# A hybrid decoder step in fp32 on one core: head sums shared between two engines, and cached values summed four units at a time

## The chip, the core and the metric

One NeuronCore of a Trainium2 chip runs the whole kernel as one program. The metric is the device time of one execution in microseconds (us). TensorE, VectorE, ScalarE, GpSimd and SyncE are the core's engines; the profile calls them PE, DVE, ACT, POOL and SP. Each runs its own list of instructions in order, and they wait for each other by semaphores alone.

## The reference

One layer of a hybrid decoder, for 256 prompt tokens and for 8 sequences of 4 new tokens that look back at 2048 cached positions each (288 tokens in all, width 2048):

```
h = rmsnorm(x);  q,k,v, qi,ki,wi, cx,cb,cc, ga,gb = split(h @ w_in)
score = sum over 16 index heads of wi * relu(qi . ki)        # picks keys
idx   = top_k(score)            # 64 for the prompt, 256 for the samples
logit[h,j] = q[h] . k[idx[j],h] / sqrt(128) + rel_bias       # 8 heads of 128
attn  = softmax(logit) @ v[idx]          # rows come from a paged cache
m = sigmoid(ga) * (attn @ w_pa) + sigmoid(gb) * ((cb * conv(cc*cx)) @ w_pb)
x = x + m @ w_o;  x = x + relu(rmsnorm(x) @ w1)**2 @ w2;  y = rmsnorm(x)
```

For the samples each of the 32 queries picks 256 keys of its own. Key rows and value rows (8 heads x 128 numbers, 4 KB) are fetched from HBM by their picked positions.

## The kernel before

**Projections.** Every fp32 product is made of three: a weight tile is split into a high half (VH, a rounded copy) and a low half (VL, the rest), the activations likewise, and TensorE adds high*high, high*low and low*high (lines 428 to 430). The input projection runs over 44 *pairs* of 256 output columns (`win_half`), each pair over eight *chunks* u of two 128-row tiles: 12 matmuls a chunk. So chunk number u runs from 0 to 351, pair p is chunks 8p to 8p+7. For each chunk SyncE loads weights into `wring`, ScalarE copies VH (`highs`, up to four chunks ahead of TensorE, line 932), and VectorE or GpSimd subtracts VL (`lows`, lines 1281 and 1834). `dve_low(u)` (line 77) says which: in the key stage VectorE has chunks 2 and 6 of eight, in the value stage the odd ones, and GpSimd the others. After the projections come the mixing, output and MLP products, which the change does not touch (there `WH` and `WL` play the same parts).

All else is hung between those chunks by hand: `win_half(p, half, after)` calls `after(j)` behind chunk j, and every other engine places its own work by `highs(end)` or `lows(end)`, "first all halves below chunk `end`, then this".

**Picking.** VectorE finds the 256 best keys of each sample query, four positions to a *unit*: 64 units, and in each of them partition 4n+s of 128 works for query n and its key s. `comb` holds positions by query. `picked` (line 707) spreads them over 128 partitions by four matmuls with the 0/1 matrices `rs`; `bias_at(0)` (line 735) does the same for the new tokens' column. VectorE turns positions into row numbers `offs` (lines 1495 to 1506).

**Key stage (pairs 15 to 30).** GpSimd gathers one unit of key rows (128 rows of 4 KB, 512 KB) into one of `RK` = 5 buffers of `kv` (`gather`, line 1843), once the unit five earlier has been read. VectorE multiplies the unit by the queries in PSUM banks 6 and 7 (`by_query`, line 1521) and sums each head's 128 products (`by_head`, line 1525) into the logits `lg`. Units are paced by `unit_end(n)` (line 73): 1.9 chunks a unit.

```
for n in range(UNITS):
    dve.wait_ge(ks[n % RK], 16 * (n // RK + 1))
    by_query(kv[:, n % RK, :])
    by_head(kv[:, n % RK, :], lg[:, n, :])
    lows(unit_end(n) + 4)
```

GpSimd's side (line 1859): `lows(unit_end(n - RK) + 4 or 5)`, then `gather(n)`. Small work of VectorE stands between units: four `one_hot`, four `gated` products, the new token's keys in `knrep` (unit 35, summed at unit 41). The prompt's own top 64 takes eight rounds of `prompt_top` (line 1486): two before the units, six in pair 31.

**Value stage (pairs 31 to 38).** After the softmax VectorE spreads each unit's probabilities into one of two tiles `sp` (`spread_unit`, line 1597), and after every second chunk TensorE multiplies two units of value rows by them (`unit_sum` and `v_unit`, lines 835 to 846): per unit 8 heads, in fp32 two passes each, so 16 small matmuls. `vnrep` (the new tokens' values) comes first. The value rows use the same five buffers. Between the halves of a pair stand the prompt's attention products, and VectorE has its softmax rows and the convolution.

Of the kernel before, what the change touches and what calls it, by code (L numbers as in the profile page):

```python
# [59 lines left out]
           ("iota", NPG), ("tpos", 1), ("nd", DT), ("lo", NB), ("npos", DT), ("par", 1)]  # L60
# [5 lines left out]
NEWKEY = 35  # L66
RAW = 3
# [5 lines left out]
def unit_end(n):  # L73
    return 8 * KP + (3 + 19 * n // 5) // 2
# [44 lines left out]
def build(nc, I, O):  # L119
    with ExitStack() as ctx:  # L120
# [54 lines left out]
        sp = sb("sp", [P, 2, H, NS])  # L175
# [89 lines left out]
        def const(name, rows=P):  # L265
# [19 lines left out]
            "unit_read conv_done soft_ready soft_turned lg_shifted lg_exp "  # L285
            "sp_ready unit_summed o_copied ot_done ot_copied "
            "ul_ready ul_turned ul_copied u_out res_add relu_raw y_turned y_copied y_squared ssy_sum root_ready y_out "
# [3 lines left out]
        ks = [ctx.enter_context(nc.semaphore(f"rows_in{i}")) for i in range(RK)]  # L291
# [8 lines left out]
        C_MLP = C_WO + 16  # L300

# [102 lines left out]
        def _(pe):  # L404
# [495 lines left out]
        def _(act):  # L900
# [258 lines left out]
            for p in range(VP, AP0 + H + 1):  # L1159
# [20 lines left out]
                if p == VP + UNITS // UNIT:  # L1180
                    act.wait_ge(S["ot_done"], 1)
                    copy(zB[:, 0:H, SEQ:TOK], bank(6, 0, H * NS).rearrange("p (h n) -> p h n", h=H)).then_inc(S["ot_copied"], 1)
            act.activation(XH[:, 0:CT, :], zB[:, CT:KT, :], ACT.Copy).then_inc(S["xh_ready"], 1)
            gate(AP0 + H + 1)
            act.wait_ge(S["ot_copied"], 1)
# [69 lines left out]
            act.wait_ge(S["ssy_sum"], 1)  # L1255
            act.activation(root3, ssq, ACT.Sqrt, bias=eps[:, 0:1], scale=1.0 / D).then_inc(S["rms_ready"], 1)
            act.wait_ge(S["root_ready"], 1)
# [11 lines left out]
        def _(dve):  # L1269
# [257 lines left out]

            dve.wait_ge(S["q_wide"], 2)
# [14 lines left out]
            for n in range(UNITS):  # L1543
                dve.wait_ge(ks[n % RK], 16 * (n // RK + 1))
                by_query(kv[:, n % RK, :])
                by_head(kv[:, n % RK, :], lg[:, n, :])
# [3 lines left out]
                elif n == 10:  # L1550
                    dve.wait_ge(S["spread_done"], 3)
                    dve.tensor_scalar(newsel[:], bank(4, 0, 1), -1.0, -OFF, ALU.add, ALU.mult).then_inc(S["newpos_read"], 1)
# [6 lines left out]
                elif n == NEWKEY + 6:  # L1559
# [3 lines left out]
                    step(dve.scalar_tensor_tensor(out=rnew, in0=qstep_k[:], scalar=QKS, in1=rnew, op0=ALU.mult, op1=ALU.add))  # L1563
                if turn < 24 and unit_end(n) > UNIT * turn + UNIT:
# [10 lines left out]
            dve.wait_ge(S["unit_read"], UNITS + 1)  # L1575
            dve.wait_ge(S["bias_copied"], 1)
# [215 lines left out]
            for e in range(2):  # L1792
# [10 lines left out]
                if e:  # L1803
                    dve.tensor_reduce(ssq, ssy, AX_X, ALU.add).then_inc(S["ssy_sum"], 1)
# [4 lines left out]
            dve.wait_ge(S["ssy_sum"], 1)  # L1809
# [5 lines left out]
            dve.scalar_tensor_tensor(out=root3, in0=half3, scalar=1.5, in1=root3, op0=ALU.add, op1=ALU.mult).then_inc(S["root_ready"], 1)  # L1815
            dve.wait_ge(S["root_ready"], 1)
# [7 lines left out]
        def _(pool):  # L1824
# [18 lines left out]
            def gather(n):  # L1843

                src, u = ("cache_k", n) if n < UNITS else ("cache_v", n - UNITS)
                if RK <= n < UNITS + RK:
                    pool.wait_ge(S["unit_read"], n - RK + 1 + (n - RK > NEWKEY + 6))
                elif n >= UNITS + RK:
                    pool.wait_ge(S["unit_summed"], u - RK + 2)
                pool.indirect_dma_start(out=kv[:, n % RK, :], out_offset=None, in_=I[src],  # L1850
                                        in_offset=bass.IndirectOffsetOnAxis(ap=offs[:, u:u + 1], axis=0)).then_inc(ks[n % RK], 16)
# [7 lines left out]
            for n in range(UNITS + RK):  # L1859
                lows(UNIT * KP + 4 + n if n < RK else unit_end(n - RK) + (5 if NEWKEY < n - RK < NEWKEY + 10 else 4))  # L1860
# [25 lines left out]
            pool.wait_ge(S["root_ready"], 1)  # L1886
# [4 lines left out]
def constants():  # L1891
# [11 lines left out]
    c["s32"] = (p[:, None] // 4 == n32[None, :])  # L1903
    c["b4"] = (p[:, None] // 4 == p[None, :] // 4)
# [77 lines left out]
```

## Time and profile before

| | us |
|---|---|
| median of 3 runs (1751.91 to 1753.06) | 1752.29 |
| the profiled execution | 1752.91 |
| its span, first to last instruction | 1751.1 |
| TensorE busy | 1722.1 |
| VectorE, ScalarE, GpSimd busy | 1050.5, 684.5, 535.1 |
| mean granted clock of TensorE | 0.995 of full |

The profile shows one execution. A matmul's record overlaps the next one's, since they are pipelined: its duration is some 0.29 us while a new one starts every 0.13 us, so rates are read from starts and counts. `<-` behind an idle time names what ended it. A window line gives, for a stretch, each engine's busy time and instruction count, the clock granted to TensorE, the busy share of the 16 DMA engines and what they moved. Measured from the span's start, the key stage is about 254 to 476 us and the value stage 483 to 640 us.

### The profile page before, as it was taken

What the parts mean: (1) busy time and instruction counts of PE and PEld (TensorE: products, weight loads), DVE (VectorE), ACT (ScalarE), POOL (GpSimd) and SP (SyncE); (2) the same over time, 40 slices, a digit from 0 to 9 for tenths busy, and PEclk for the clock granted to TensorE, in tenths of its full rate; (3) what the DMA queues carried; (4) which work ended last, traced back from release to release, by engine and by line L of the source; (5) the groups of instructions that cost most, each with busy time, mean ns of one, the idle gap of its engine ahead of it and who ended that gap; (6) DMA issues with size and microseconds to landing.
All of it is one profiled execution on the core that took longest, in us unless ns stands there. A gap on an engine that the chain in (4) does not pass through costs nothing.

```text
span 1751.1 us, 32532 instructions
## 1 busy us (share of the span) xinstructions
PE 1722.1 (98%) x13708; PEld 1684.4 (96%) x13708; DVE 1050.5 (60%) x1185; ACT 684.5 (39%) x846; POOL 535.1 (31%) x430
## 2 busy tenths in 40 slices
PE   9999999999999999999999999999999999999997
PEld 9879999999989999999999999999999999999997
DVE  5979999799897422555556544455444554445444
ACT  5544443434435555333333332233333333333342
POOL 1647788898967668000340000000000000000000
PEclk9999999999999999999999999999999999999998
DMA  8635558998979965644454444444444444444442
GB/s 314 208 95 181 175 179 304 347 335 309 315 264 344 325 233 155 224 168 164 159 184 166 168 167 159 160 163 168 168 167 161 159 163 166 168 169 162 154 165 103
DMA packets 74816, 351.86 MB, mean 201 GB/s; under 512 B 8978, under 2 KB 11154, under 8 KB 53684
## 3 DMA queue, kind: packets, MB, share of 16 engines
q1 hardware_dynamic: 50352, 269.05, 45.2%
q0 software_dynamic: 19584, 71.31, 11.5%
q10 hardware_dynamic: 4772, 9.95, 1.7%
q8 instruction: 81, 1.33, 0.3%
q14 instruction: 27, 0.22, 0.0%
HBM read 343.84 MB, written 6.44 MB: 200 GB/s over the span
## 4 chain that ended last, share of the span: by engine, by line
PE 81%; DVE 15%; POOL 1%; DMA 1%; issue 1%; ACT 0%; ACTq 0%; DVEq 0%
PE PM L448 20%; PE PM L450 19%; PE PM L449 19%; PE PM L428 6%; PE PM L429 6%; PE PM L430 6%; DVE ix L1464 2%; DVE scw L1466 2%; DVE scw L1463 2%; PE PM L410 2%; PE PM L838 2%; DVE kv L1523 1%; DVE VL L1287 1%; DVE lg L1526 1%; POOL kv L1850 1%
## 5 line engine op out<-in xcount | busy, mean ns | idle before, releaser
L905 ACT ACTIVATE WH<-wring 128x2048 fp32r<-128x2048 f32 (+1 forms) x163 | 307.3, 1885 | 679.9 <-PE PM L450 676.1
L1693 DVE TENSOR_TENSOR WL<-wring,WH 128x2048 fp32r<-128x2048 f32 x159 | 364.5, 2292 | 341.0 <-ACT WH L905 341.0
L1840 POOL TENSOR_TENSOR VL<-wring,VH 128x512 fp32r<-128x512 f32 x273 | 358.0, 1320 | 160.7 <-ACT VH L905 157.2
L428 PE MATMUL PM<-hH,VH 128*128 128x288 f32 x1312 | 398.2, 304 | 7.8 <-DVE VL L1287 4.4
L429 PE MATMUL PM<-hL,VH 128*128 128x288 f32 x1312 | 388.5, 296 | 0.0
L430 PE MATMUL PM<-hH,VL 128*128 128x288 f32 x1312 | 387.0, 295 | 0.0
L448 PE MATMUL PM<-XH,WH 128*128 128x288 f32 x1280 | 379.1, 296 | 1.5 <-DVE WL L1700 1.5
L449 PE MATMUL PM<-XL,WH 128*128 128x288 f32 x1280 | 377.6, 295 | 0.0
L450 PE MATMUL PM<-XH,WL 128*128 128x288 f32 x1280 | 376.3, 294 | 0.0
L448 PE MATMUL PM<-YH,WH 128*128 128x288 f32 x1264 | 374.6, 296 | 0.0
L449 PE MATMUL PM<-YL,WH 128*128 128x288 f32 x1264 | 372.9, 295 | 0.0
L450 PE MATMUL PM<-YH,WL 128*128 128x288 f32 x1264 | 371.6, 294 | 0.0
L905 ACT ACTIVATE VH<-wring 128x512 fp32r<-128x512 f32 x352 | 221.4, 631 | 319.8 <-PE PM L430 311.4
L428 PEld LDWEIGHTS PM<-hH,VH 128*128 128x128 f32 x1312 | 247.1, 188 | 18.2 <-issue 7.8
L1888 POOL TENSOR_SCALAR ysam<-ysam,small 32x512 f32<-32x512 f32 x1 | 2.4, 2372 | 823.0 <-DVE small L1815 823.0
L430 PEld LDWEIGHTS PM<-hH,VL 128*128 128x128 f32 x1312 | 248.3, 189 | 0.0
L429 PEld LDWEIGHTS PM<-hL,VH 128*128 128x128 f32 x1312 | 247.8, 189 | 0.2
L448 PEld LDWEIGHTS PM<-XH,WH 128*128 128x128 f32 x1280 | 239.8, 187 | 1.8 <-ACT G L993 1.7
L450 PEld LDWEIGHTS PM<-XH,WL 128*128 128x128 f32 x1280 | 241.1, 188 | 0.0
L449 PEld LDWEIGHTS PM<-XL,WH 128*128 128x128 f32 x1280 | 240.3, 188 | 0.1
L450 PEld LDWEIGHTS PM<-YH,WL 128*128 128x128 f32 x1264 | 238.1, 188 | 0.0
L449 PEld LDWEIGHTS PM<-YL,WH 128*128 128x128 f32 x1264 | 237.3, 188 | 0.0
(293 smaller groups left out, 1704.6 us busy)
## 6 DMA issues: line engine op xcount, KB each, us to landing
wring<-w_in SPq DMA_DIRECT2D x176, 512.0 KB, 4.6
wring<-w_mlp_in SPq DMA_DIRECT2D x64, 1024.0 KB, 5.2
wring<-w_mlp_out SPq DMA_DIRECT2D x64, 1024.0 KB, 5.2
wring<-w_o SPq DMA_DIRECT2D x16, 1024.0 KB, 5.2
wring<-w_pb SPq DMA_DIRECT2D x8, 1024.0 KB, 4.8
wring<-w_pa SPq DMA_DIRECT2D x8, 1024.0 KB
xT<-x_t SPq DMA_DIRECT2D x1, 2304.0 KB, 11.1
kv<-x_prompt SPq DMA_DIRECT2D x2, 1024.0 KB, 8.3
```

What stands on the lines that cost most here:

```text
L410: return pe.transpose(out, in_, cp[0:n, 0:n])
L428: pe.matmul(out, vh, th[:, k, :], start=(k == 0), stop=False)
L429: pe.matmul(out, vh, tl[:, k, :], start=False, stop=False)
L430: m = pe.matmul(out, vl, th[:, k, :], start=False, stop=(k == KT - 1))
L448: pe.matmul(out, wh, rh[:, k0 + k, :], start=(first and k == 0), stop=False)
L449: pe.matmul(out, wh, rl_[:, k0 + k, :], start=False, stop=False)
L450: m = pe.matmul(out, wl, rh[:, k0 + k, :], start=False, stop=(last and k == CK - 1))
L838: m = pe.matmul(PM[q:q + NS, 6, c:c + HD], sp[:, ring, h, :], rows[:, h * HD:h * HD + HD], start=(first and h < 4), stop=False, skip_group ...
L905: return act.activation(out, in_, ACT.Copy, **kw)
L1463: step(dve.max(v8, sc2))
L1693: dve.tensor_tensor(WL[:, i % 2], wring[:, i % 2], WH[:, i % 2], ALU.subtract).then_inc(S["wl_ready"], 1)
L1840: pool.tensor_tensor(VL[:, u % 4], r, VH[:, u % 4], ALU.subtract).then_inc(S["vl_pool"], 1)
```

## The change

1. **Heads shared.** For the 28 units 5, 7, ..., 59 (`SHARED`) VectorE multiplies the half with heads 4 to 7 first, then the half with heads 0 to 3, and sums only heads 0 to 3. ScalarE sums heads 4 to 7 by four copies with accumulation, placed behind the VH copy of chunk `unit_end(n) + 4`. A gather over such a unit waits for ScalarE too.
2. **Prompt tops** 2 to 7 move from pair 31 to units 6, 9, 12, 15, 18 and 21.
3. **Spreading** of `comb` by one matmul with `rall` (all four positions to all partitions) instead of four with `rs`; VectorE then picks each partition's own with a 0/1 constant `sel` and a sum.
4. **Gathers** follow `lows(unit_end(n - RK) + 6)`; the first eight follow one chunk each.
5. **Values** are summed four units at a time, after chunks 3 and 7 of a pair, with four `sp` tiles and seven row buffers: the five of `kv`, `knrep` and `vnrep`.
6. Some semaphores are merged (`norm_step`, `o_copied`).

```diff
+SHARED = range(5, 60, 2)
+TOPS_AT = (6, 9, 12, 15, 18, 21)
-        sp = sb("sp", [P, 2, H, NS])
+        sp = sb("sp", [P, 4, H, NS])
+        def v_row(v):
+            r = v % (RK + 2)
+            if r < RK:
+                at = (UNITS + r) % RK
+                return kv[:, at, :], ks[at], 16 * (-(-(UNITS - at) // RK) + v // (RK + 2) + 1)
+            return (knrep if r == RK else vnrep)[:], ks[r], 16 * (v // (RK + 2) + 1)
 # TensorE
-                    for s in range(4):
-                        m = pe.matmul(bank(4, 0, UNITS), const("rs", NS)[:, s * P:s * P + P], comb[:, 0:UNITS, s],
-                                      start=(s == 0), stop=(s == 3))
-                    m.then_inc(S["spread_done"], 1)
+                    pe.matmul(bank(4, 0, TOPK), const("rall", NS), comb[:, 0:UNITS, :].rearrange("p u s -> p (u s)"),
+                              start=True, stop=True).then_inc(S["spread_done"], 1)
...
-                    for s in range(4):
-                        m = pe.matmul(bank(4, 0, 1), const("rs", NS)[:, s * P:s * P + P], comb[:, UNITS, s:s + 1],
-                                      start=(s == 0), stop=(s == 3))
-                    m.then_inc(S["spread_done"], 1)
+                    pe.matmul(bank(4, 0, 4), const("rall", NS), comb[:, UNITS, :],
+                              start=True, stop=True).then_inc(S["spread_done"], 1)
...
             def v_unit(v):
-                n = UNITS + v
+                rows, arrived, count = v_row(v)
                 pe.wait_ge(S["sp_ready"], v + 2)
-                pe.wait_ge(ks[n % RK], 16 * (n // RK + 1))
-                unit_sum((1 + v) % 2, kv[:, n % RK, :])
+                pe.wait_ge(arrived, count)
+                unit_sum((1 + v) % 4, rows)
...
-                    if j % 2 and v < UNITS:
-                        v_unit(v - 1)
-                        v_unit(v)
+                    if j == 3 and v < UNITS:
+                        for i in range(4):
+                            v_unit(v - 3 + i)
 # ScalarE
+            def unit_heads(n):
+                act.wait_ge(S["unit_made"], SHARED.index(n) + 1)
+                for h in range(H // 2, H):
+                    row = kv[:, n % RK, h * HD:h * HD + HD]
+                    m = act.activation(row, row, ACT.Copy, accum_out=lg[:, n, h:h + 1])
+                m.then_inc(S["unit_act"], 1)
+            shared_at = {unit_end(n) + 4: n for n in SHARED}
             def highs(end):
...
                     copy(VH[:, u % 4], raw[u // 2 % 4][:, 2 * (u % 2):2 * (u % 2) + 2, :]).then_inc(S["vh_ready"], 1)
+                    if u in shared_at:
+                        unit_heads(shared_at[u])
 # VectorE
-            pw = bank(4, 0, UNITS)
+            pw, every = bank(4, TOPK, UNITS), view(scw, 0, [UNITS, 4])
+            step(dve.tensor_tensor(every, bank(4, 0, TOPK).rearrange("p (u s) -> p u s", s=4),
+                                   const("sel").unsqueeze(1).to_broadcast([P, UNITS, 4]), ALU.mult))
+            step(dve.tensor_reduce(pw, every, AX_X, ALU.add))
...
+            def half_unit(rows, out):
+                for e in (1, 0):
+                    part = rows[:, 512 * e:512 * e + 512]
+                    m = dve.tensor_tensor(part, part, PM[:, 6 + e, :], ALU.mult)
+                    if e:
+                        m.then_inc(S["unit_made"], 1)
+                    else:
+                        step(m)
+                dve.tensor_reduce(out, rows[:, 0:512].rearrange("p (h d) -> p h d", h=H // 2), AX_X, ALU.add).then_inc(S["unit_read"], 1)
...
-                by_query(kv[:, n % RK, :])
-                by_head(kv[:, n % RK, :], lg[:, n, :])
+                if n in SHARED:
+                    half_unit(kv[:, n % RK, :], lg[:, n, 0:H // 2])
+                else:
+                    by_query(kv[:, n % RK, :])
+                    by_head(kv[:, n % RK, :], lg[:, n, :])
                 lows(unit_end(n) + 4)
...
+                if n in TOPS_AT:
+                    prompt_top(2 + TOPS_AT.index(n))
...
-                if v:
-                    dve.wait_ge(S["unit_summed"], v)
-                spread((1 + v) % 2, lg[:, v, :].unsqueeze(2).to_broadcast([P, H, NS]))
+                if v >= 3:
+                    dve.wait_ge(S["unit_summed"], v - 2)
+                spread((1 + v) % 4, lg[:, v, :].unsqueeze(2).to_broadcast([P, H, NS]))
...
-                    if c % 2 == 0 and v < UNITS:
-                        spread_unit(v)
-                        spread_unit(v + 1)
+                    if c % 4 == 0 and v < UNITS:
+                        for i in range(4):
+                            spread_unit(v + i)
                     lows(UNIT * p + c + 4)
                     if p == VP:
-                        if c < TOPP // 8 - 2:
-                            prompt_top(c + 2)
 # GpSimd
             for n in range(UNITS + RK):
-                lows(UNIT * KP + 4 + n if n < RK else unit_end(n - RK) + (5 if NEWKEY < n - RK < NEWKEY + 10 else 4))
+                lows(UNIT * KP + 4 + n if n < RK + 3 else unit_end(n - RK) + 6)
                 gather(n)
...
-            for v in range(0, UNITS - RK):
-                lows(UNIT * VP + v + 5)
-                gather(UNITS + RK + v)
+            for v in range(RK, UNITS):
+                if v == RK:
+                    pool.wait_ge(S["unit_read"], UNITS + 1)
+                else:
+                    lows(UNIT * VP + v - 2)
+                    pool.wait_ge(S["unit_summed"], v - RK)
+                gather_v(v)
```

## Rows read from the trace of the kernel before

**Rows 1.** Page, busy us (share of the span) xinstructions
```profile
PE 1722.1 (98%) x13708; PEld 1684.4 (96%) x13708; DVE 1050.5 (60%) x1185; ACT 684.5 (39%) x846; POOL 535.1 (31%) x430
```

**Rows 2.** Waits of TensorE, whole run: us in total, times, longest
```profile
PE PM L428 <- DVE VL L1287: 5.4, 5, 2.4
PE PM L428 <- POOL VL L1840: 3.0, 3, 2.2
PE PM L838 <- DVE sp L1595: 2.6, 4, 0.8
```

**Rows 3.** Windows: us, busy (x) of each engine, PEclk, DMA share, GB/s
```profile
430.00:455.66 25.66, 25.66 (x194) 25.66 (x194) 23.66 (x22) 11.21 (x18) 23.69 (x21) 1.00 0.92 321
547.44:566.65 19.21, 19.21 (x236) 17.65 (x235) 8.23 (x20) 9.91 (x17) 12.98 (x13) 1.00 0.92 327
```

**Rows 4.** Windows of TensorE alone: us, busy (x), PEclk, DMA share, GB/s
```profile
260.00:270.00 10.00, 6.90 (x45) 0.96 0.90 304
270.00:280.00 10.00, 10.00 (x69) 0.87 0.96 341
390.00:400.00 10.00, 9.07 (x67) 1.00 0.91 320
400.00:410.00 10.00, 9.40 (x71) 1.00 0.87 304
410.00:420.00 10.00, 8.24 (x50) 0.83 0.85 279
470.00:480.00 10.00, 8.93 (x66) 1.00 0.89 315
```

**Rows 5.** Timeline of TensorE, value stage: start us, us, engine line op
```profile
498.29 1.08 PE L838 MATMUL PM<-kv,sp 128*32 128x128 f32 x32 [0.82 <-DVE sp L1595]
...
547.22 0.29 PE L430 MATMUL PM<-hH,VL 128*128 128x288 f32 x1
547.44 1.08 PE L838 MATMUL PM<-kv,sp 128*32 128x128 f32 x32
548.45 0.40 PE L428 MATMUL PM<-hH,VH 128*128 128x288 f32 x1
```

**Rows 6.** Timeline of TensorE's weight loads, same visit
```profile
547.44 0.81 PEld L838 LDWEIGHTS PM<-kv,sp 128*32 128x32 f32 x32 [0.17 <-issue]
```

**Rows 7.** Timeline of VectorE, key stage and value stage
```profile
316.31 0.69 DVE L1287 TENSOR_TENSOR VL<-wring,VH 128x512 fp32r<-128x512 f32 x1 [1.80 <-ACT VH L905]
316.92 1.22 DVE L1523 TENSOR_TENSOR kv<-kv,PM 128x1024 f32<-128x1024 f32 x1
318.17 1.22 DVE L1526 TENSOR_REDUCE lg<-kv 128x8 f32<-128x1024 f32 x1
...
488.37 0.28 DVE L1489 MAX8 m8p<-mask 128x8 f32<-128x128 f32 x1
...
490.05 0.29 DVE L1489 MAX8 m8p<-mask 128x8 f32<-128x128 f32 x1
...
511.68 0.41 DVE L1614 TENSOR_REDUCE qstep<-scw 128x1 f32<-128x256 f32 x1
```

**Rows 8.** Timeline of ScalarE, value stage
```profile
512.12 0.40 ACT L1145 ACTIVATE scw<-scw,qstep 128x128 f32<-128x128 f32 x1 [1.39 <-DVE qstep L1614]
...
512.52 0.49 ACT L1145 ACTIVATE scw<-scw,qstep 128x256 f32<-128x256 f32 x1
```

**Rows 9.** Timeline of GpSimd, key stage
```profile
267.32 1.27 POOL L1840 TENSOR_TENSOR VL<-wring,VH 128x512 fp32r<-128x512 f32 x1
...
304.89 0.96 POOL L1850 DMA_INDIRECT kv<-cache_k,offs  x1
```

**Rows 10.** Timeline of TensorE, the two blocks that spread `comb`
```profile
245.51 1.18 PE L711 MATMUL PM<-comb,cp 32*128 32x64 f32 x8
...
286.23 1.05 PE L740 MATMUL PM<-comb,cp 32*128 32x1 f32 x8
```

**Rows 11.** Gathers of line 1850, from issue to landing
```profile
DMA to landing us min/median/max: 4.8/6.7/9.0
```

More of the change, by code:

```diff
@@ L59 @@
 CONST_P = [("ident", P), ("rs", 4 * P), ("rall", P), ("s32", NS), ("b4", P), ("ok4", 4),
-           ("iota", NPG), ("tpos", 1), ("nd", DT), ("lo", NB), ("npos", DT), ("par", 1)]
+           ("iota", NPG), ("tpos", 1), ("nd", DT), ("lo", NB), ("npos", DT), ("par", 1), ("sel", 4)]
 CONST_E = [("onehot", TW), ("amask", DB * P), ("causal", 3 * P), ("pgsel", P), ("r8", 1)]
@@ L284, in build @@
             "plog_done plog_read pmax_ready pexp_done pprob_ready pt_turned pt_copied po_done po_copied "
-            "unit_read conv_done soft_ready soft_turned lg_shifted lg_exp "
-            "sp_ready unit_summed o_copied ot_done ot_copied "
-            "ul_ready ul_turned ul_copied u_out res_add relu_raw y_turned y_copied y_squared ssy_sum root_ready y_out "
+            "unit_read unit_made unit_act conv_done soft_ready soft_turned lg_shifted lg_exp "
+            "sp_ready unit_summed o_copied ot_done "
+            "ul_ready ul_turned ul_copied u_out res_add relu_raw y_turned y_copied y_squared norm_step y_out "
             "ptT_in ptT_ready prow_sum prow_ready wh_ready wl_ready xh_ready xl_ready yh_ready yl_ready mix_sum dve_step "
@@ L290, in build @@
         ld = [ctx.enter_context(nc.semaphore(f"weights_in{i}")) for i in range(RING)]
-        ks = [ctx.enter_context(nc.semaphore(f"rows_in{i}")) for i in range(RK)]
+        ks = [ctx.enter_context(nc.semaphore(f"rows_in{i}")) for i in range(RK + 2)]
         pages_in = [ctx.enter_context(nc.semaphore(f"pages_in{i}")) for i in range(DB)]
@@ L1181, in _ @@
                     act.wait_ge(S["ot_done"], 1)
-                    copy(zB[:, 0:H, SEQ:TOK], bank(6, 0, H * NS).rearrange("p (h n) -> p h n", h=H)).then_inc(S["ot_copied"], 1)
+                    copy(zB[:, 0:H, SEQ:TOK], bank(6, 0, H * NS).rearrange("p (h n) -> p h n", h=H)).then_inc(S["o_copied"], 1)
             act.activation(XH[:, 0:CT, :], zB[:, CT:KT, :], ACT.Copy).then_inc(S["xh_ready"], 1)
             gate(AP0 + H + 1)
-            act.wait_ge(S["ot_copied"], 1)
+            act.wait_ge(S["o_copied"], 2)
             act.wait_ge(S["po_copied"], H)
@@ L1254, in _ @@
                 half_squares(e)
-            act.wait_ge(S["ssy_sum"], 1)
+            act.wait_ge(S["norm_step"], 1)
             act.activation(root3, ssq, ACT.Sqrt, bias=eps[:, 0:1], scale=1.0 / D).then_inc(S["rms_ready"], 1)
-            act.wait_ge(S["root_ready"], 1)
+            act.wait_ge(S["norm_step"], 2)
             act.wait_ge(S["y_copied"], 8)
@@ L1551, in _ @@
                     dve.wait_ge(S["spread_done"], 3)
-                    dve.tensor_scalar(newsel[:], bank(4, 0, 1), -1.0, -OFF, ALU.add, ALU.mult).then_inc(S["newpos_read"], 1)
+                    step(dve.tensor_tensor(m8[:, 0:4], bank(4, 0, 4), const("sel"), ALU.mult))
+                    step(dve.tensor_reduce(m8[:, 4:5], m8[:, 0:4], AX_X, ALU.add))
+                    dve.tensor_scalar(newsel[:], m8[:, 4:5], -1.0, -OFF, ALU.add, ALU.mult).then_inc(S["newpos_read"], 1)
                     dve.wait_ge(S["newpos_read"], 1)
@@ L1575, in _ @@
             dve.wait_ge(S["unit_read"], UNITS + 1)
+            dve.wait_ge(S["unit_act"], len(SHARED))
             dve.wait_ge(S["bias_copied"], 1)
@@ L1803, in _ @@
                 if e:
-                    dve.tensor_reduce(ssq, ssy, AX_X, ALU.add).then_inc(S["ssy_sum"], 1)
+                    dve.tensor_reduce(ssq, ssy, AX_X, ALU.add).then_inc(S["norm_step"], 1)
                 m = dve.tensor_tensor(ynat[:, :, c], bank(6).rearrange("p (q n) -> p q n", q=2)[:, :, h],
@@ L1808, in _ @@
                     m.then_inc(S["y_copied"], 1)
-            dve.wait_ge(S["ssy_sum"], 1)
+            dve.wait_ge(S["norm_step"], 1)
             dve.wait_ge(S["rms_ready"], 3)
@@ L1814, in _ @@
             step(dve.tensor_tensor(half3, half3, root3, ALU.mult))
-            dve.scalar_tensor_tensor(out=root3, in0=half3, scalar=1.5, in1=root3, op0=ALU.add, op1=ALU.mult).then_inc(S["root_ready"], 1)
-            dve.wait_ge(S["root_ready"], 1)
+            dve.scalar_tensor_tensor(out=root3, in0=half3, scalar=1.5, in1=root3, op0=ALU.add, op1=ALU.mult).then_inc(S["norm_step"], 1)
+            dve.wait_ge(S["norm_step"], 2)
             dve.wait_ge(S["y_copied"], 8)
@@ L1843, in gather, with gather_v @@
             def gather(n):
[L1845 to L1851, printed above, removed]
+                if n >= RK:
+                    k = n - RK
+                    pool.wait_ge(S["unit_read"], k + 1 + (k > NEWKEY + 6))
+                    if k in SHARED:
+                        pool.wait_ge(S["unit_act"], SHARED.index(k) + 1)
+                if n < UNITS:
+                    pool.indirect_dma_start(out=kv[:, n % RK, :], out_offset=None, in_=I["cache_k"],
+                                            in_offset=bass.IndirectOffsetOnAxis(ap=offs[:, n:n + 1], axis=0)).then_inc(ks[n % RK], 16)
+                else:
+                    gather_v(n - UNITS)
+            def gather_v(v):
+                rows, arrived, _ = v_row(v)
+                pool.indirect_dma_start(out=rows, out_offset=None, in_=I["cache_v"],
+                                        in_offset=bass.IndirectOffsetOnAxis(ap=offs[:, v:v + 1], axis=0)).then_inc(arrived, 16)
             for b in range(DB):
@@ L1864, in _ @@
                     pool.memset(up[:, :, 0:2], 0.0).then_inc(S["pads_zero"], 1)
[L1865 to L1867 removed]
+            for v in range(RK, UNITS):
+                if v == RK:
+                    pool.wait_ge(S["unit_read"], UNITS + 1)
+                else:
+                    lows(UNIT * VP + v - 2)
+                    pool.wait_ge(S["unit_summed"], v - RK)
+                gather_v(v)
             lows(C_MIX)
@@ L1885, in _ @@
             square_pairs(0, 0)
-            pool.wait_ge(S["root_ready"], 1)
+            pool.wait_ge(S["norm_step"], 2)
             pool.wait_ge(S["y_copied"], 8)
@@ L1903, in constants @@
     c["s32"] = (p[:, None] // 4 == n32[None, :])
+    c["sel"] = (p[:, None] % 4 == np.arange(4)[None, :])
     c["b4"] = (p[:, None] // 4 == p[None, :] // 4)
```

## The prediction

> **What bounds the kernel now.** I read the totals first: TensorE is busy 1722.1 of 1751.1 us [rows 1], so all that can be won is a gap between its instructions, or fewer or cheaper instructions. The second view is who waited for whom, TensorE's part: its longest totals are 5.4 us for VectorE's low halves VL, 3.0 us for GpSimd's, 2.6 us for the spread tiles `sp` [rows 2]. Third come its windows. A clean stretch, 430.00 to 455.66, holds 194 matmuls in 25.66 us, 132 ns each [rows 3]. Against that beat of 75.6 matmuls per 10 us the key stage has three holes [rows 4]:
> - its start, 260 to 280 us: 114 matmuls, not 151, so some 4.9 us lost;
> - its middle, 390 to 420 us: 188, not 227: 5.1 us;
> - its end, 470 to 480 us: 66: 1.3 us.
>
> A hole costs more than its wait: the granted clock fell to 0.87 in 270 to 280 and 0.83 in 410 to 420 [rows 4], below the full 2.4 GHz, after waits of up to 2.2 and 2.4 us [rows 2].
>
> **Value stage: groups of four.** A visit to two units is 32 small matmuls: the last projection matmul starts at 547.22, the units at 547.44, the next projection matmul at 548.45 [rows 5]. Against a beat of 0.13 the way in costs 0.09; the way out costs 0.11 (that next matmul ran 0.40, a clean one 0.29); the visit itself 1.01. Of that 1.01, 0.81 is the 32 weight loads back to back [rows 6]; 0.20 is a tail in which nothing issues. So the fixed part is 0.40 us a visit. There are 32 visits of two and there will be 16 of four: 16 x 0.39 = **6.2 us** gained. Were the tail owed by each unit, only the ways in and out would go: 16 x 0.20 = 3.2, my lower bound; nothing supports more than 6.4.
> The rows show the fixed part. The Trainium skill (TensorEngine Tiling (Array Packing), Key Properties) says that changing the tiling mode drains TensorE; by it, a pair of mode changes per visit is what is halved, which gives the 6.2 and not the 3.2.
>
> **Value stage: the waits for `sp`.** Twice before two-unit visits it waited 0.82 us, as at 498.29 [rows 5], and twice inside one, 0.5 each; 2.6 in all [rows 2], plus two tails of a split visit, 0.2 each. They come from six `prompt_top` calls, 1.68 us each (488.37 to 490.05) [rows 7], put between the spreads. Those leave this stage, and with four `sp` buffers the spreads of a group are made while the previous group's four chunks run, some 6 us early. I take **2.8 us**; bounds 2.0 and 3.0. The 1.1 us wait for VL right after the new key's rows stays: four spreads now stand ahead of that subtraction, not two, but the third and fourth fit into the time that the new key's matmuls take.
>
> **Key stage: VectorE.** A unit is a product of 1.22 and a sum of 1.22 us, starting 1.25 apart and 2.39 together [rows 7]. Of 28 units it now makes two half products (a subtraction of 128x512 took 0.69, 0.61 to its successor) and half a sum (128x256 took 0.41 [rows 7], so 128x512 some 0.68, 0.60 issued). That is 0.60 + 0.64 + 0.60 = 1.84: 0.54 saved, 15 us in all. Against it, six tops x 1.71 = 10.3 us move in at units 6 to 21. There VectorE has room: it waits for VH, 1.80 us per two units [rows 7], some 13 us from unit 10 to 24. So the tops are hidden; if that cover were gone they would show as a wait for VL. From unit 23 on, before the middle hole, ten shared units give 5 us, where VectorE was late by 2.4. But gathers are issued two chunks later, and one crowded stretch may eat the lead. I take 1.5 us of the hole as left if so: **3.4 us** gained, bounds 0 and 5.1. At the end VectorE comes 1 us sooner to the softmax: **1.2** of 1.3; bounds 0.5 and 1.3.
>
> **Key stage: ScalarE.** Four sums of 128x128 with accumulation: one, with its read-out, occupied 0.40 us (512.12 to 512.52) [rows 8], so 1.6 us per shared unit, 45 us in 178. ScalarE is 44% busy there (11.21 of 25.66 us) [rows 3]; it becomes about 70%. Queued behind the new wait and sums are the next VH, and behind that GpSimd's and VectorE's VL and TensorE. In 16 chunks of 1.60 us it idles 14.45, 0.9 a chunk, so the next VH comes 0.7 us late, with an evacuation 1.2. VH is made four chunks (6.4 us) ahead, and copy and subtraction need 2, so it is covered. The wait itself ends in time where VectorE is no more than 3 us behind.
>
> **Key stage: GpSimd.** It is the fullest helper: 23.69 of 25.66 us [rows 3]. Its gathers now come after VL two chunks further on. At the start that helps: before, three gathers in a row stood ahead of the VL at 267.32 [rows 9] for which TensorE waited 2.2 us. But all of it starts 0.9 us later: two new operations on 128x256 and 256-to-64 elements (0.43 + 0.45 from the 0.41 of [rows 7]) stand before the row numbers, and TensorE arrives 0.6 us sooner. Following both queues, chunks 125 to 129 each wait 0.6 to 0.9 us for GpSimd and chunk 130 some 2 us for VectorE, which is also 0.9 us late: 7 us lost where 5 were. Term: **-2.0**, bounds -4 and +3.
>
> **Matrix products merged.** Eight passes took 1.18 us busy (1.11 to the next) and 1.05 (0.97) [rows 10]. One matmul of two passes instead: 0.5 for 256 columns, 0.3 for 4. **1.2 us**; bounds 0.6 and 1.6.
>
> **Gathers.** Issued some 3.3 us later, against a lead of 11 us for unit 17 (issued at 304.89 [rows 9], used at 316.92 [rows 7]) and somewhat less later, with landings of 4.8 to 9.0, median 6.7 [rows 11]: VectorE will wait for rows more often, with 3 us before TensorE feels it. In the value stage seven buffers hold one group and three units more, so a burst of four keeps the queue filled. The two new rows are `knrep` and `vnrep`, free by then. For these and small collisions I charge **-1.0** (0 to -4). The renamed semaphores and the last norm cost nothing: the same waits.
>
> **Sum.** 6.2 + 2.8 + 3.4 + 1.2 - 2.0 + 1.2 - 1.0 = 11.8 us. Against the profiled execution (1752.91: span 1751.1 and 1.8 around it) that is 1741.1; it lay 0.6 above the median, so 1740.5. A measurement here tells about 0.2%, 3.5 us, from no change.
>
> **The rivals.**
> - *The tail is per unit* (0.11): 3.0 us less, **1743.5**. Against it: the loads run back to back through both units [rows 6].
> - *The transfers become the bound of the value stage* (0.11). A pair there moves 2.10 MB of weights and 4.19 MB of rows: 327 GB/s at share 0.92 over 19.21 us [rows 3]; full share would be 355, 17.7 us. I ask for 19.2 - 0.8 = 18.4 us, 342 GB/s. If late rows take half of what the groups win, **1744**; the sign would be waits on `kv`, `knrep` or `vnrep`. The Trainium skill (DMA: Bandwidth & Descriptors, Bandwidth) puts a core's HBM share at about 358 GB/s; by that the pair could not be under 17.6 us, still short of a bound.
> - *The start gains from the new order* (0.10): GpSimd's delay matters less than I think, the 2.2 us wait and its slow clock go, and the middle hole closes: **1734**.
> - *Slower: ScalarE's wait for VectorE's half product* (0.07). Place: the VH copy behind each of the 28 waits, at chunk `unit_end(n) + 4`. If rows land so late that the product ends over 3 us after VH, TensorE stops at each: 0.6 us of wait and 0.2 of restart, 28 x 0.8 = 22 us, against 11.8 + 1.0 of gain: **1762**. It decides from about 0.45 us a unit. For it: the later gathers; against: the latest that VectorE has been cost TensorE 2.4 us [rows 2], and it will be earlier.
> - *The sharing does nothing* (0.05), since TensorE waits for VectorE in few places: then groups, `sp` waits and merged products remain less the start: **1744**.
>
> **The numbers.** Forecast 0.56. All but the slower one lie at 1734 to 1744. The range, 1733 to 1747, takes in the start and the middle at their bounds, not the slower rival. Faster by over 0.2% means under 1748.8: 0.88; within: 0.05; slower 0.07.
>
> **What would show it.** Right: value-stage visits of 64 matmuls in about 1.8 us, 18.4 us a pair, no wait for `sp`; one row of ScalarE sums at 0.40; a smaller middle hole; a start with several waits under 1 us. Wrong: waits on ScalarE's VH in the key stage, DMA waits on the rows, or visits of 2.0 us.

## The result, and the profile after

The changed kernel takes **1755.64 us** (median of 20 runs, 1752.96 to 1757.55), the kernel before 1752.55 in the same comparison: ratio 1.0016, 95% interval 1.0010 to 1.0022. I had forecast 1740.5. The profiled execution lies at 1754.53, its span is 1752.7.

**Where the time went.** ScalarE copies each VH at a fixed place in TensorE's work, so the start of the same copy in two traces shows how far one kernel is ahead at a chunk. The changed one against before, in us (+ is behind):

| from chunk to chunk | what lies there | forecast | measured |
|---|---|---|---|
| 112 to 124, 136 to 144 | the two merged products | -1.2 | -0.5, -0.9 |
| 124 to 136 | start of the key stage | +2.0 | +3.9 |
| 144 to 244 | rest of it, the middle hole | -3.4 | -0.8 |
| 244 to 256 | softmax, hand-over | -1.2 | +3.4 |
| 256 to 316 | value stage | -9.0 | -2.8 |

(The -1.0 charged for the gathers belongs to the third line and the last; the changed one was 0.6 us ahead already at chunk 112. The misses: 6.2 us in the value stage, 4.6 at the hand-over from the key stage to it, 2.6 and 1.9 before.) The page's busy times, TensorE's waits [rows 2] and its windows [rows 4]:

```profile
PE 1719.8 (98%) x13696; PEld 1685.7 (96%) x13696; DVE 1068.3 (61%) x1217; ACT 713.6 (41%) x1070; POOL 534.4 (30%) x430
```
```profile
PE PM L438 <- DVE VL L1305: 11.9, 8, 3.6
PE PM L438 <- POOL VL L1877: 2.0, 4, 0.7
```
```profile
260.00:270.00 10.00, 7.74 (x55) 1.00 0.93 323
270.00:280.00 10.00, 6.43 (x39) 0.83 0.88 307
390.00:400.00 10.00, 7.82 (x47) 0.83 0.88 320
...
410.00:420.00 10.00, 10.00 (x77) 1.00 0.89 291
...
480.00:490.00 10.00, 8.21 (x62) 0.83 0.57 197
```

The waits for `sp` are gone, but those for VectorE's VL have grown from 5.4 to 11.9 us. The start is worse (39 matmuls in 270 to 280, there were 69), the middle hole has only moved from 409 to 391 (its wait is 2.2 us, it was 2.4), and there is a new one at 480. The granted clock is at 0.83 in each of the three. The four longest waits in the timeline of TensorE, and a visit of four units:

```profile
274.64 0.40 PE L438 MATMUL PM<-hH,VH 128*128 128x288 f32 x1 [3.57 <-DVE VL L1305]
...
393.74 0.40 PE L438 MATMUL PM<-hH,VH 128*128 128x288 f32 x1 [2.18 <-DVE VL L1305]
...
482.84 0.40 PE L438 MATMUL PM<-hH,VH 128*128 128x288 f32 x1 [1.79 <-DVE VL L1305]
...
542.71 0.40 PE L438 MATMUL PM<-hH,VH 128*128 128x288 f32 x1 [1.46 <-DVE VL L1305]
...
582.43 1.96 PE L844 MATMUL PM<-kv,sp 128*32 128x128 f32 x64
584.31 0.70 PE L820 MATMUL PM<-scw,G 128*128 128x256 f32 x2
```

What VectorE did just before each, from its timeline:

```profile
272.35 2.24 DVE L1305 TENSOR_TENSOR VL<-wring,VH 128x512 fp32r<-128x512 f32 x1
...
390.31 3.37 DVE L1305 TENSOR_TENSOR VL<-wring,VH 128x512 fp32r<-128x512 f32 x1
...
479.91 2.87 DVE L1305 TENSOR_TENSOR VL<-wring,VH 128x512 fp32r<-128x512 f32 x1
...
538.90 3.16 DVE L1634 TENSOR_TENSOR sp<-cp,lg 128x256 f32<-128x256 f32 x4
541.98 0.68 DVE L1305 TENSOR_TENSOR VL<-wring,VH 128x512 fp32r<-128x512 f32 x1
```

And GpSimd at the same times:

```profile
271.54 2.49 POOL L1877 TENSOR_TENSOR VL<-wring,VH 128x512 fp32r<-128x512 f32 x2
...
390.63 2.49 POOL L1877 TENSOR_TENSOR VL<-wring,VH 128x512 fp32r<-128x512 f32 x2
...
479.71 2.52 POOL L1877 TENSOR_TENSOR VL<-wring,VH 128x512 fp32r<-128x512 f32 x2
...
540.48 1.28 POOL L1877 TENSOR_TENSOR VL<-wring,VH 128x512 fp32r<-128x512 f32 x1
```

There is one pattern in these rows. A VL of VectorE takes 0.69 us [rows 7]; where it is *held*, that is, stands beside one of GpSimd's without getting on, it takes what is left of GpSimd's and then its own. Three times GpSimd has two back to back, and VectorE gets nothing between them: the VL begun at 390.31 ends at 393.68, 0.56 after GpSimd's second. At 538.90 four spreads (1.43 us when free) are held behind the VL at 540.48, and VectorE's VL stands behind them.

### The profile page after: what moved, and what is told of

Read it like the earlier page. It is cut to its first block, busy times and chain, and to the rows that moved or that the text cites. A ratio compares the mean times of both kernels' runs of the same rounds, so it can differ in the third digit from the quotient of the medians.

```text
span 1752.7 us, 32795 instructions
## 1 busy us (share of the span) xinstructions
PE 1719.8 (98%) x13696; PEld 1685.7 (96%) x13696; DVE 1068.3 (61%) x1217; ACT 713.6 (41%) x1070; POOL 534.4 (30%) x430
## 4 chain that ended last, share of the span: by engine, by line
PE 80%; DVE 16%; DMA 1%; issue 1%; ACT 1%; POOL 1%; ACTq 0%; another core or an unknown queue 0%; DVEq 0%
PE PM L458 20%; PE PM L460 19%; PE PM L459 19%; PE PM L438 6%; PE PM L440 6%; PE PM L439 6%; DVE ix L1482 2%; DVE scw L1484 2%; DVE scw L1481 2%; PE PM L420 1%; DVE VL L1305 1%; PE PM L844 1%; DMA kv<-cache_k,offs 1%; DVE mask L1413 1%; DVE lg L1547 1%
```

## The experiments

Theories after the result: **A**, the groups bring what I forecast and something on VectorE eats it; **B**, a visit of 64 small matmuls is worth less than I thought. After the first four runs A became: VectorE's operations stand still while GpSimd subtracts. Times are medians; before lay at 1752.2 to 1752.5 in every comparison.

**1. The value stage alone (`v4`), and with visits of two (`v2`).** `v4` is the kernel before with `sp` [P, 4, ..], `v_row`, `gather_v`, the four spreads and the visits of four; `v2`:

```
-                    if j == 3 and v < UNITS: four v_unit
+                    if j % 2 and v < UNITS:  v_unit(v - 1); v_unit(v)
```

> The kernel before with the value stage of the change alone: groups of four, four `sp`, seven row buffers; key stage, tops in pair VP and spreads by eight or four passes as before. Theory A (the value stage brings what I forecast, the key stage ate it): 9 us faster than before, 1743.5. Theory B (a visit of 64 small matmuls leaves gaps behind it, so that a group of four saves 0.15 us and not 0.39; 16 x 0.15 = 2.4, plus 2.8 for the `sp` waits, less one collision of 1.5): 3 to 5 us faster, 1748.5, with the gaps of 0.1 to 0.25 us in the first 12 projection matmuls after most visits, as in the changed kernel.

> The same, but visits of two units after j = 1 and j = 3 (four `sp` and seven row buffers stay). It tells what the grouping by itself is worth. Theory A: 6.2 us slower than the kernel with groups of four. Theory B: 1 to 3 us slower than it, no gaps after visits, 2 to 3 us faster than before (the `sp` waits).

`v4` 1753.5 (ratio 1.0006, 0.9997 to 1.0015), `v2` 1752.1. Both expectations failed: the whole value stage brought nothing. But B's sign did not appear either: behind the visits of `v4` stand only the 0.1 to 0.2 us of before. From chunk 280 to 316 `v4` gains 3.0 us in nine visits, 0.34 each. All of it and more is given back in two waits for VL, 2.9 and 2.4 us (timelines of VectorE and GpSimd ahead of the second; when free four `zB` take 1.8 us and four spreads 1.43):

```profile
533.71 3.31 DVE L1656 SCALAR_TENSOR_TENSOR zB<-uv,gcol,zB 128x256 f32<-128x256 f32 x4
...
537.72 3.15 DVE L1603 TENSOR_TENSOR sp<-cp,lg 128x256 f32<-128x256 f32 x4
540.80 0.68 DVE L1295 TENSOR_TENSOR VL<-wring,VH 128x512 fp32r<-128x512 f32 x1
```
```profile
535.40 1.32 POOL L1848 TENSOR_TENSOR VL<-wring,VH 128x512 fp32r<-128x512 f32 x1
...
539.31 1.27 POOL L1848 TENSOR_TENSOR VL<-wring,VH 128x512 fp32r<-128x512 f32 x1
```

**2. No sharing in the changed kernel (`noshare`): `SHARED = ()`.**

> The changed kernel without the sharing: VectorE sums all 16 heads of every unit, ScalarE none; everything else as changed (tops at units 6 to 21, gathers later, value stage in fours). Theory A (the sharing helps, collisions are chance): VectorE falls behind by 0.54 us a unit, the middle hole grows by 4 us or more, 1758 to 1762. Theory B (it is the sharing's and the tops' shift of VectorE against GpSimd that makes the waits): the hole of the middle is as before or up to 2 us more, 1755 to 1757. If the wait before the value stage (3.6 us at 480) goes, sharing caused it.

1758.4, within theory A's range and 2.8 us slower than the changed kernel. So the sharing helps within the change, though the stretch from chunk 144 to 244 lost 2.5 us by its absence and not 4. The wait at the hand-over is there without it too (1.9 us), so it isn't the sharing's.

**3. The key stage's gathers where they were (`oldorder`).**

```
-                lows(UNIT * KP + 4 + n if n < RK + 3 else unit_end(n - RK) + 6)
+                lows(UNIT * KP + 4 + n if n < RK else unit_end(n - RK) + (5 if NEWKEY < n - RK < NEWKEY + 10 else 4))
```

> The changed kernel with the gathers of the key stage at the chunks of the kernel before (unit_end + 4 or + 5, the first five at chunk 124 to 128). Theory A (the later gathers cost 1 us and save at the start): the start loses what it lost before or 1 us less than changed; VectorE's waits for rows in 320 to 400 go; 1753 to 1756. Theory B (the later gathers are what makes VectorE late from 320 on and moves the hole to 377 and 391): the middle hole shrinks by 3 us, 1751 to 1753. Theory C (the start's 5 us come from the two new operations and from VectorE and GpSimd colliding, not from the order): chunk 130 still waits 2 us or more for VectorE.

1753.2, in theory A's range; theory B falls, for chunk 144 to 244 loses 1.9 us. The start costs 0.9 instead of 3.4 (chunk 112 to 136), and theory C falls: with three gathers in a row at 264 GpSimd subtracts nothing while VectorE makes its first `one_hot` (0.68 us, in the changed kernel 1.49). Later GpSimd waits 15.5 us in ten places for ScalarE's sums before it may gather. TensorE waits 13 times for GpSimd's VL in the whole run, 8.5 us; four of these waits, 4.0 us, belong to the start.

**4. VL before the spreads (`v4_vlfirst`, `after_vlfirst`, `old_vlfirst`), and two spreads and two (`v4_split`).**

```
+                    lows(UNIT * p + c + 4)
                     if c % 4 == 0 and v < UNITS: four spreads      # v4_split: c % 4 < 2, two spreads
-                    lows(UNIT * p + c + 4)
```

> The kernel with the value stage of the change alone (`v4`, 1753.5), in which VectorE now makes its VL before the four spreads, not behind them. Theory A (the gain of the groups, some 0.33 us a visit, is eaten by two waits for that VL: 2.9 and 2.4 us, with the slower clock behind them 8.5 us in all, since four spreads, up to 3.2 us when GpSimd works at the same time, stand ahead of it): both waits go and it takes 1745 to 1747. Theory B (VectorE is too full there whatever the order): the waits for VL turn into waits for `sp`, 1751 to 1754.

> The same, with two spreads behind the VL at c = 0 mod 4 and two behind c = 1 mod 4. Theory A: no different from all four behind VL by more than 1.5 us, since both leave VL free. If it is the length of the burst that matters and not the order, this one is the better by 1 to 3 us.

> The changed kernel, whole, with only that order changed. Its value stage has one wait for VL of 1.5 us (loss 1.7); theory A: 1.5 to 3 us faster than changed, 1753 to 1754. The start (3.7 us worse than before) and the wait at the hand-over to the value stage (3.6) stay. Theory B: no gain, 1755 to 1756.

> The changed kernel with the key stage's gathers at their old chunks (`oldorder`, 1753.2) and VL before the spreads. Theory A: its two waits for VL in the value stage (2.3 and 1.1 us, 5.2 us lost in all) go, 1747 to 1749, below both kernels. Theory B: 1752 to 1754.

1752.6, 1750.9, 1753.9 and 1752.4: 0.9, 2.6, 1.7 and 0.8 us under the same kernels without it. Only `after_vlfirst` gains what was expected; `v4_vlfirst` ends 5.6 and `old_vlfirst` 3.4 us above their ranges. Two spreads and two beat four in a row by 1.7 us, just over the 1.5 that the expectation allowed to theory A. The order was a small part; other operations of VectorE were held in its place (in `v4_split` two additions to the mask, 2.18 us where 0.6 is their time, ahead of a wait of 1.5 us at 508).

**5. GpSimd subtracts nothing in the value stage from its fifth chunk, 252, on (`v4_nopool`, `after_nopool`).** The decisive pair. In `v4_nopool` (from `v4_split`) and `after_nopool` (the changed kernel and nothing else):

```
-    return ... or VP <= p < VP + 8 and j % 2 == 1
+    return ... or VP <= p < VP + 8 and (j % 2 == 1 or u > 8 * VP + 3)
```

> `v4_split` (1750.9), in which VectorE makes every VL of the value stage from its fifth chunk on and GpSimd none, so that the two never subtract at the same time. Theory A (VectorE's operations with both inputs in SBUF stand still while GpSimd subtracts: 18 us held in 490 to 580 and 13 in 580 to 640 in `v4_split`): the held time of those stretches falls under 3 us, one VL keeps to 0.69, the waits for VL from 500 on go, and although VectorE has 28 more subtractions (28 x 0.61 = 17 us) it is faster by 2 to 4 us: 1747 to 1749. Theory B (VectorE is simply full): the added 17 us make it late, 1752 to 1757.

> The changed kernel (1755.6) with that alone: the spreads stand ahead of VL as changed. Theory A: the wait of 1.5 us at 541 goes, the held time of 490 to 640 falls from 32 us to under 4, and visits of four bring 0.33 us each from the first on: 1751 to 1753. If the small gaps behind its visits (0.2 to 0.6 us each, until 577) come of GpSimd's work too, they go with it; if they stay, they have another cause. Theory B: 1755 to 1758.

`v4_nopool` **1744.5** (ratio 0.9956, 0.9942 to 0.9969), `after_nopool` **1747.4** (0.9974, 0.9963 to 0.9985): 8.3 us off the changed kernel by giving VectorE more work. Both are faster than theory A had expected (1747 to 1749, and 1751 to 1753). Groups by line and form of VectorE from 490 to 640 us (busy, mean ns), of before, changed and `after_nopool`:

```profile
L1287 DVE TENSOR_TENSOR VL<-wring,VH 128x512 fp32r<-128x512 f32 x30 | 21.6, 721 | 0.0
...
L1612 DVE TENSOR_TENSOR scw<-scw,mask 128x384 f32<-128x384 f32 x7 | 4.8, 685 | 0.2
...
L1609 DVE SCALAR_TENSOR_TENSOR scw<-PM,G 128x256 f32<-128x256 f32 x7 | 2.9, 412 | 0.0
```
```profile
L1634 DVE TENSOR_TENSOR sp<-cp,lg 128x256 f32<-128x256 f32 x63 | 35.3, 594 | 30.7 <-PE PM L844 15.8 <-remote 14.9
L1305 DVE TENSOR_TENSOR VL<-wring,VH 128x512 fp32r<-128x512 f32 x32 | 29.3, 918 | 2.0 <-issue 1.3 <-ACT VH L911 0.6
L1651 DVE TENSOR_TENSOR scw<-scw,mask 128x384 f32<-128x384 f32 x7 | 14.0, 2006 | 0.2
```
```profile
L1305 DVE TENSOR_TENSOR VL<-wring,VH 128x512 fp32r<-128x512 f32 x59 | 40.6, 690 | 38.6 <-ACT VH L911 38.4
L1634 DVE TENSOR_TENSOR sp<-cp,lg 128x256 f32<-128x256 f32 x60 | 22.7, 422 | 3.9 <-PE PM L844 3.7
...
L1651 DVE TENSOR_TENSOR scw<-scw,mask 128x384 f32<-128x384 f32 x8 | 4.5, 558 | 0.3
L1648 DVE SCALAR_TENSOR_TENSOR scw<-PM,G 128x256 f32<-128x256 f32 x8 | 3.3, 414 | 0.0
```

The mask addition went from 685 to 2006 ns with the change and to 558 without GpSimd beside it; VL 721, 918, 690. The operation that reads PSUM (`scw<-PM,G`) stays at 409 to 414. Adding up what each row took over the shortest of its form in the run, VectorE stood still for some 14 us of 490 to 640 in before, 38 changed, 1 in `after_nopool`; it is busy 93.8 us there against 112.3 (windows), with 27 more subtractions. That rows might come sooner, now that GpSimd has time for its gathers, isn't the reason: TensorE waits for no rows there in either trace. In `after_nopool` it has no wait in that stage at all. From one visit to the same one a pair later it takes 18.93 us in the changed kernel (the pair shown; others 18.5 to 19.0) and 18.55 in `after_nopool`; before it was 19.21 [rows 3]. So a pair gains 0.66 us, not the 0.8 that I had forecast:

```profile
563.50:582.43 18.93, 18.93 (x237) 17.86 (x236) 12.41 (x20) 9.83 (x17) 13.01 (x12) 1.00 0.92 333
```
```profile
574.42:592.97 18.55, 18.55 (x237) 17.72 (x236) 10.64 (x24) 9.92 (x17) 9.40 (x8) 1.00 0.97 344
```

From chunk 256 to 316 `after_nopool` gains 8.2 us over before, 5.3 more than the changed kernel. Going from visit to visit, these 5.3 have two parts. Some 2.4 us lie between the visits at 533 and 544: the wait of 1.46 us for VL, and a visit that took 2.28 us and not 1.88. The other 3 come in steps of 0.7 us or less at most of the other visits. They are small gaps, of 0.1 to 0.25 us each, between projection matmuls. In `after_nopool` they are gone, but the profile names no engine that ended them, so their mechanism is open. In `v4`, which has none of these gaps, the two intervals with a wait for VL are 4.5 and 3.8 us longer than in `after_nopool`: 8.3 of the 8.8 us between the two traces from the first visit of four to the last. There the held operations account for nearly all.

The traces of changed and `after_nopool` differ by 3 us more where the two programs are the same: at the hand-over and in the middle, waits of the same length (1.8 and 2.18 us) cost 2.1 and 2.4 us, in the changed kernel's trace 3.6 and 4.0. The granted clock goes with it: 0.57 from 394 to 398 in the changed kernel's trace, 1.00 in the other. The medians have the whole 8.3; how much of those 3 us they hold is open.

**6. The same with the old gathers (`old_nopool`), and three of eight VL for VectorE in the key stage (`old_third`: `j in (1, 4, 6)` from pair 18).**

> The changed kernel with the old chunks for the key stage's gathers, two spreads and two behind VL, and VectorE alone for VL in the value stage. Theory A: value stage 9 us shorter than before as I forecast, the key stage 2 us longer than before (as in `oldorder` at 470): 1745 to 1748. Theory B: 1751 to 1754.

> The same, and from pair 18 on VectorE makes three of eight VL of the key stage, not two (12 x 0.61 = 7 us more for it, 12 x 1.3 = 16 us less for GpSimd), paid for by the sharing. If the eight waits of 0.2 to 1.2 us for GpSimd's VL in `oldorder` from 353 to 465 are GpSimd's own load, they go: 3 us faster than `old_nopool`. If VectorE has no room even with the sharing, it waits for VectorE's VL instead and is 2 to 6 us slower.

1746.9 and 1747.5. The first is as A expected. The second is neither 3 us faster nor 2 slower: TensorE's waits for GpSimd's VL fell from 9.2 to 6.6 us, those for VectorE's grew from 1.3 to 5.1 (1.1 us at 358, 1.7 at 404).

**7. The pieces of the key stage on `v4_nopool` (1744.5).**

> `v4_nopool` (1744.5) with the merged products and VectorE's two added operations alone. TensorE gains 1.3 us (0.5 at 245, 0.7 at 285), the row numbers come 0.9 us later. If the start loses no more than that 0.9: 1743.5 to 1745. If the 0.9 us turns into collisions as in the changed kernel's start: 1746 to 1748.

> `v4_nopool` with the sharing of 28 key units alone (tops in pair 31, spreads and gathers as before). If the 0.54 us saved per shared unit reaches TensorE, the middle hole (2.4 us wait at 408, 0.6 at 424) goes: 3 to 4 us faster, 1741. If ScalarE's sums make row buffers free later, so that GpSimd issues gathers late and is late with its VL, the waits for GpSimd of 0.2 to 1.2 us from 353 to 465 of `old_nopool` are there too and it is 0 to 3 us slower, 1745 to 1747.

> `old_nopool` (1746.9) with the prompt tops back in pair 31: sharing and merged products, no moved tops. If the moved tops (10.3 us of VectorE in units 6 to 21) are what makes the waits from 353 on, it is 2 to 4 us faster, 1743 to 1745; if the sharing is, 1746 to 1748.

> `after_nopool` (1747.4) with GpSimd's VL up to chunk 250 ahead of the gather into `knrep`. If that gather pushes GpSimd's two subtractions onto VectorE's VL, they start 0.9 us earlier, VectorE's VL is held 0.9 to 1.5 us less and the wait of 1.8 us shrinks to under 1: 1745.5 to 1747. If not, 1747 to 1748.

`merge_alone` 1744.3, `share_alone` 1746.8, `share_merge` 1747.6 (against 1746.9 with the tops moved), `handover` 1747.6 (against 1747.4). So the merged products and the moved tops come to nothing either way (under 1 us), and the sharing with the old gathers *costs* 2.3 us. GpSimd's waits in 280 to 470 us of `share_alone` (the profiled execution took 1751.8, the longest of its six; in `share_merge`, profiled at 1747.1, they are 18.3 us), and TensorE's in the whole of `share_merge`, four of them, 4.1 us, at the start:

```profile
POOL kv L1887 <- ACT kv L943: 17.5, 10, 3.2
```
```profile
PE PM L438 <- POOL VL L1877: 8.6, 13, 2.2
```

A shared unit frees its buffer only when ScalarE has summed it; GpSimd waits for that with its VL queued behind. In `handover` GpSimd's VL up to chunk 250 stand ahead of its gather into `knrep`. The wait of 1.8 us for VL at the hand-over went, and one of 0.8 us for `scw` came; the stretch from chunk 244 to 256 was 1.2 us shorter in the trace, but the total doesn't show it.

**8. All together (`mix`), and with the tops in pair 31 (`mix_tops31`).** `mix` is all of the change, with VectorE alone for VL in the value stage, its spreads two and two behind VL, GpSimd's VL ahead of the gather into `knrep`, and the first gathers early:

```
+                lows(UNIT * KP + 4 + n if n < RK else unit_end(n - RK) + (4 if n < RK + 3 else 6))
```

> All of the change; gathers of units 0 to 7 at the old chunks, later ones two chunks later as changed; VectorE alone for VL in the value stage, its four spreads two and two behind VL; GpSimd's VL before the gather into `knrep`. If the start's loss is that order alone, it loses 0.5 to 1 us at the start, like `oldorder`, not 3.4; the key stage from 280 to 470 gains 1 to 2 us over before, as in `after_nopool`; 1743 to 1745, the best of all by 0 to 1.5 us. If the late gathers after an early start bring new waits, 1746 to 1748.

> The same with the prompt tops in pair 31, where they were before. VectorE has 10 us more room in units 6 to 21 and 10 us less in pair 31, where v4_nopool lost 0.7 us by a wait for VL. 0 to 1 us slower than `mix` if that wait is all; faster by 1 to 2 us if the tops are what leaves a hole at 378 and 391.

1744.6 and 1745.1. Both totals are as expected. The start loses 2.1 us (chunk 112 to 136), between `oldorder`'s 0.9 and the change's 3.4: the order of those gathers is about half of it, not all. The key stage from 148 to 244 gains 0.7, not 1 to 2. Holes stay at 376 and 390, with the tops there or not. There VectorE comes late from waits for rows, since the later gathers that spare GpSimd its wait take the lead from the rows (VectorE's waits for the gathers in the whole run, before, changed and `mix`):

```profile
DVE kv L1523 <- DMA kv<-cache_k,offs: 3.7, 3, 2.5
```
```profile
DVE kv L1544 <- DMA kv<-cache_k,offs: 7.8, 5, 3.1
```
```profile
DVE kv L1544 <- DMA kv<-cache_k,offs: 8.0, 4, 2.8
```

`v4_nopool`, `merge_alone` and `mix` can't be told apart (1744.3 to 1744.6); all three beat the kernel before by 7.7 us or more and the changed one by 11. The simplest, `v4_nopool`, has no sharing at all.

## Why the prediction was wrong

- **"Value stage: groups of four"**: the mechanism was right, the term a little large: 0.33 to 0.34 us a visit where nothing is held (16 x 0.335 = 5.4, not 6.2). The visit of 64 takes 1.88 us, not 1.82 (582.43 to 584.31, last rows of TensorE's timeline above).

- **"the waits for `sp`"**: gone, and worth their 2.8 by subtraction: the 8.2 of `after_nopool` less 5.4. But in the changed kernel all of it was lost again. The step that failed is the one behind it: that VectorE's operations have constant durations, whatever stands beside them, so that more of them in a row "fit". I took VectorE's durations from free rows and its room from idle time, and charged 1.0 for "small collisions". Four spreads in a row were held for up to 1.7 us, and VL behind them. Of the 6.2 us missed in the value stage, 5.3 go when GpSimd doesn't subtract there: 2.4 are the held spreads and the disturbed visit before them, some 3 the small gaps, whose mechanism is open. Outside that stage the same step shows in the rows above: the waits of 3.6, 2.2 and 1.8 us at the start, in the middle and at the hand-over stand each behind a held VL (2.24, 3.37 and 2.87 us for 0.69). No run with GpSimd's subtractions taken out of the key stage tests that part.
- The rule bears it out in part: the Trainium skill (SBUF — State Buffer, Who interferes with whom) says that a VectorE instruction with two SBUF inputs contends with a GpSimd instruction that reads SBUF, and that whoever issues first gets the shared ports for the whole instruction while the other blocks fully. The trace agrees on what is held and how fully: VL, `sp`, mask and `zB` by up to 2.7 us, those with an input in PSUM (409 to 414 ns) never; of the 64 products of `by_query` in `v4`, 58 ran at least in part beside a subtraction of GpSimd and none took longer (1.21 to 1.22 us). It doesn't bear out the order as the records give it: the VL begun at 390.31 was held by subtractions begun at 390.63. I costed each operation by itself and left this rule out, though it is the one that spoke against the change.
- **"Key stage: VectorE"**: the half products and sum took what I said (1.28 for two, 0.69), and the tops were hidden, as `share_merge` shows. What failed is "3.4 us gained": the saved time went into waits for rows (VectorE's 7.8 us, there were 3.7), and the hole came at 391 instead of 409, with a VL held for 2.7 us. How much it cost differs by execution: from chunk 144 to 244 the changed kernel's trace gained 0.8 us, that of `after_nopool`, the same program up to there, 2.3. That is also the **"Gathers"** term, -1.0: the sign was right, but these waits moved the hole rather than adding to it. "End: 1.2" failed wholly: VectorE did not come 1 us sooner (TensorE's wait for `small` in the softmax was 0.9 us, there were 1.1), and its VL fell on top of GpSimd's two, pushed there by the gather into `knrep`. By `handover` that collision is worth 1.2 us in the trace.
- **"Key stage: ScalarE"**: cheaper than said, about 1.17 us a unit, not 1.6 (timeline; the next starts 0.29 later), and TensorE never waited for VH in it. That half of the slower rival is refuted. But "covered, so nothing" missed who waits for the *sums*: with gathers at the old chunks GpSimd does, 17.5 us.

```profile
318.10 0.29 ACT L939 ACTIVATE kv<-kv 128x128 f32<-128x128 f32 x1
318.30 0.19 ACT L939 ACTIVATION_READ_ACCUMULATOR kv<-kv 128x1 f32 x1
318.39 0.29 ACT L939 ACTIVATE kv<-kv 128x128 f32<-128x128 f32 x1
```

- **"Key stage: GpSimd"**: the pattern came as forecast, three waits of 0.6 for GpSimd and then one for VectorE's VL at chunk 130, but that was 3.6 us and not 2, because this VL (2.24 us for 0.69) and a `one_hot` before it (1.49 for 0.68) were held, and one of 1.1 for that `one_hot` came too; -3.9, inside my bound of -4 only just.
- **"Matrix products merged"**: 1.4 measured (0.5 and 0.9), right; worth nothing in the total (`merge_alone`), presumably since the row numbers come later by nearly as much.
- **The rivals**: the transfers did not bind: TensorE waited for no rows in the value stage, though at 344 GB/s and share 0.97 in the pair of 18.55 little room is left. None of my signs of failure showed; the failure had no rival. All my cases took VectorE's durations as they stood in the trace before.

## What to carry to other kernels

Before you count on an engine's idle time, compare in the trace each form's mean with its shortest row: where VectorE's operations with both inputs in SBUF are longer beside GpSimd's, the two queues share a resource, and a change of phase between them can re-deal the waits. Giving all such work of a stage to one engine made it less busy here (93.8 us for 112.3), though it had more to do. And test a change's stages one by one: here a gain of 8 us was real and hidden behind a collision that a one-line change removed.

## What the hardware showed that I had not expected

- A held VectorE operation doesn't get in between two back-to-back subtractions of GpSimd: 3.37 us for a VL of 0.69, beside an `x2` of 2.49.
- Which of the two is held can't be read from their starts. In the changed kernel's trace eight VL of VectorE were held to the end of a subtraction that began 0.1 to 0.5 us after them, while three went through in 0.68 with one beginning 0.4 to 0.6 after. GpSimd's own took under 1.35 us in 258 of 273 cases. What decides is open.
- Not only operations with two inputs are held: the scaling of 128x128 (`scw<-scw,qstep`, 0.29 us free) took 1.37 and 1.51 beside a subtraction in the changed kernel.
- Behind visits of 64 there are in some kernels small gaps between projection matmuls, up to 0.7 us a visit (`v4_split`, `v4_vlfirst` and the changed kernel, there mostly until 577), in `v4` with the same TensorE program as the first two none. In all kernels in which GpSimd doesn't subtract there they are gone. What makes them is open.
- The same program up to chunk 244 (`v4`, `v2`, `v4_vlfirst`, `v4_split`, `v4_nopool`) went from chunk 112 to there in -0.1, +0.6, +0.4, -1.3 and -1.7 us against before, in one execution each: waits of 2.35 us lost 2.6 or 4.1, depending on whether the granted clock fell behind them (windows of TensorE behind that wait in `v4_split` and in `v4_nopool`). So a stage's gain under 1.5 us is not to be read from one profile of each kernel.

```profile
412.00:416.00 4.00, 4.00 (x23) 0.67 0.89 305
```
```profile
412.00:416.00 4.00, 4.00 (x32) 1.00 0.91 306
```
